# Four channel groups of a depthwise convolution moved from banded matmuls on TensorE to fp32 taps on VectorE

## The reference

```
def conformer_conv_branch(h, w_in, w_dw, b_dw, g_ln, b_ln, w_o):
    a, bgl, g = jnp.split(h @ w_in, 3, axis=-1)
    u = a * jax.nn.sigmoid(bgl)
    u = lax.conv_general_dilated(u, w_dw, window_strides=(1,), padding=[(CONV_PAD, CONV_PAD)], ...,
                                 feature_group_count=CONV_W) + b_dw
    u = jax.nn.silu(layer_norm(u, g_ln, b_ln)) * jax.nn.silu(g)
    return u @ w_o
```

## Time and profile before

| | us |
|---|---|
| median of 3 runs (lowest to highest) | 3001.74 (3001.47 to 3002.21) |
| span of the profiled execution | 2998.3 |
| its TensorE busy | 2915.5 |
| its VectorE busy | 1813.3 |
| its ScalarE busy | 1451.9 |
| its POOL busy | 426.1 |

### The profile page before, as it was taken

One profiled execution on the slowest core, in us unless ns is written; L12 is line 12 of the kernel. 1 busy time (PEld: TensorE's weight loads), 2 busy tenths in 40 slices (PEclk: granted clock), 3 DMA queues, 4 the chain that ended last, 5 costly groups with the idle time before them and its releaser, 6 DMA issues. The chain is left out here.

```text
span 2998.3 us, 44473 instructions
## 1 busy us (share of the span) xinstructions
PE 2915.5 (97%) x14789; PEld 2434.0 (81%) x14789; DVE 1813.3 (60%) x3147; ACT 1451.9 (48%) x3080; POOL 426.1 (14%) x491
## 2 busy tenths in 40 slices
PE   6999999999999999999999999999899999999898
PEld 4888888788888888888888888788788888888687
DVE  6555654567777677776767676733534444445875
ACT  5554645455555565656555565534512222222553
POOL 0000000022212221222122221200011111112000
PEclk9999999999999999999999999999999999999899
DMA  7657565611112111110212011145522222222563
GB/s 268 209 194 267 177 205 176 212 56 44 52 43 75 36 46 59 59 58 27 72 43 75 27 39 57 63 170 179 192 73 76 78 77 65 77 64 89 174 201 124
DMA packets 225865, 320.67 MB, mean 107 GB/s; under 512 B 81760, under 2 KB 143728, under 8 KB 224752
## 3 DMA queue, kind: packets, MB, share of 16 engines
q1 hardware_dynamic: 221040, 309.57, 31.7%
q10 hardware_dynamic: 4608, 8.39, 0.7%
HBM read 220.24 MB, written 97.66 MB: 106 GB/s over the span
## 5 line engine op out<-in xcount | busy, mean ns | idle before, releaser
L1309 DVE TENSOR_TENSOR at_ptlo<-at_T,at_pthi 128x512 fp32r<-128x512 f32 x576 | 396.6, 689 | 304.3 <-ACT at_pthi L1187 301.4
L1171 ACT ACTIVATE at_prob<-at_S,at_nmax 128x512 f32<-128x512 f32 x634 | 407.5, 658 | 341.4 <-DVE at_nmax L1285 334.5
L1187 ACT ACTIVATE at_pthi<-at_T 128x512 fp32r<-128x512 f32 x576 | 349.0, 608 | 210.1 <-PE at_T L1053 210.0
L1274 DVE TENSOR_REDUCE at_mx<-at_S 128x1 f32<-128x512 f32 x634 | 390.1, 629 | 73.2 <-PE at_S L1026 70.1
L1053 PE MATMUL at_T<-ident,at_prob 128*128 128x128 f32 x2304 | 346.1, 273 | 4.1 <-DVE at_ptlo L1309 4.1
L1053 PEld LDWEIGHTS at_T<-ident,at_prob 128*128 128x128 f32 x2304 | 279.4, 140 | 69.6 <-DVE at_ptlo L1309 12.8
L182 PE MATMUL ci_ps<-h1hi,ci_whi 128*128 128x512 f32 x768 | 300.2, 391 | 5.3 <-DVE h1lo L1970 5.3
L183 PE MATMUL ci_ps<-h1lo,ci_whi 128*128 128x512 f32 x768 | 299.7, 390 | 0.0
L184 PE MATMUL ci_ps<-h1hi,ci_wlo 128*128 128x512 f32 x768 | 299.4, 390 | 0.0
L182 PE MATMUL at_O<-at_pthi,at_vhi 128*128 128x512 f32 x576 | 270.1, 469 | 0.6 <-DVE at_og L1323 0.5
L1021 PE MATMUL at_S<-at_khi,at_qhi 128*128 128x512 f32 x634 | 245.3, 387 | 13.9 <-ACT at_prob L1171 10.9
(11 more groups left out here) (288 smaller groups left out, 6132.3 us busy)
## 6 DMA issues: line engine op xcount, KB each, us to landing
fr_w<-in_w_front SPq DMA_DIRECT2D x75, 512.0 KB, 4.4
at_wmod<-in_w_mod SPq DMA_DIRECT2D x32, 512.0 KB, 3.3
cv_w<-in_cv_w_in SPq DMA_DIRECT2D x24, 512.0 KB, 4.3
fr_w<-in_w_front SPq DMA_DIRECT2D x24, 384.0 KB, 4.1
values<-fr_ob SPq DMA_DIRECT2D x36, 256.0 KB, 3.2
at_vst<-values SPq DMA_DIRECT2D x8, 1152.0 KB, 7.0
fr_w_mod<-in_w_modr SPq DMA_DIRECT2D x17, 512.0 KB, 5.3
fr_x<-in_x SPq DMA_DIRECT2D x16, 512.0 KB, 6.8
```

The costliest lines, as they stand in the source:

```text
L1171: nc.scalar.activation(prob[:, j % 2, i, k], bank(h, j, i, c)[:, 0:k.stop - k.start], ACT.Exp, scale=SCALE, bias=nmax[:, i % 2:i % 2 + 1], ...
L1187: nc.scalar.activation(dst, T[:, (n + SLOTS * j) % 2], ACT.Copy).then_inc(s_hi, 1)
L1274: nc.vector.tensor_reduce(mx[:, i % 2, c:c + 1], bank(h, j, i, c)[:, 0:k.stop - k.start], AXX, ALU.max).then_inc(s_mx, 1)
L1309: nc.vector.tensor_tensor(ptlo[:, kt % 3], T[:, (n + SLOTS * j) % 2], pthi[:, kt % 3].bitcast(F32), ALU.subtract).then_inc(s_lo, 1)
```

## The change

Groups 0, 1, 3 and 4 (`TAPPED`) are no longer convolved by TensorE. Their u is loaded whole from DRAM into `ci_ut` (128 channels by 8 phases by 256 columns, with two columns of zeros on each side), and VectorE adds up 31 taps in `ci_acc`: one TENSOR_SCALAR for the first tap with the bias, then SCALAR_TENSOR_TENSOR, acc = u * weight + acc. A shift by a number of tokens that is no multiple of 8 wraps around the phases, so a tap is two instructions, together 2048 elements a partition. Each tap waits for the semaphore of the one before it. There are one `ci_ut` and one `ci_acc`.

`TAP_STEPS` deals out the 124 taps over the twelve steps of bodies 1 to 6: 20 or 21 a body, one or two a step, behind everything else that VectorE does in the step. A finished group is stored (`store_acc`), and the next is loaded directly behind (`load_rows`); the next group's first tap waits for both. The groups' sums are made in bodies 3, 4, 6 and 7 (`SUMMED_IN`), from rows reloaded from DRAM chunk by chunk (`reload_z`, `ci_zr`), with the same three operations as before.

Groups 2, 5, 6 and 7 (`BY_PE`) stay as they were, in bodies 3, 6, 7 and the tail of 7. Where a banded and a tapped group are summed in the same body, their sums alternate, and ScalarE's square stands between. `ci_gb` is gone: gates and u share `ci_ub`. All loops are written out. No other stage changes.

```
+TAPPED = (0, 1, 3, 4)
+SUMMED_IN = (3, 4, 6, 7)
+TAP_STEPS = [(g, s, n) for a, row in ((1, (1, 2, 2, 1, 2, 2, 1, 2, 2, 1, 2, 2)), (2, (1, 2, 2, 2, 2, 2, 1, 2, 2, 1, 2, 2)), (
+    3, (1, 2, 2, 1, 2, 2, 2, 2, 2, 1, 2, 2))) for g in (a, a + 3) for s, n in enumerate(row)]
...
+            def load_rows(i):
+
+                g = TAPPED[i]
+                for k in range(2):
+                    sp.wait_ge(s_ust[k], g * 32 + 32)
+                if i:
+                    sp.wait_ge(s_tap, i * CONV_K)
+                sp.dma_start(ut[:, :, HALO:HALO + NCOL], net.u_phases[g]).then_inc(s_ut, 16)
+
+            def store_acc(i):
+                sp.wait_ge(s_tap, (i + 1) * CONV_K)
+                sp.dma_start(net.z_phases[TAPPED[i]], acc[:]).then_inc(s_acc, 16)
+
+            def reload_z(i, q):
+
+                n = i * CH + q
+                if q == 0:
+                    sp.wait_ge(s_acc, 16 * (i + 1))
+                if n >= 2:
+                    sp.wait_ge(s_d, at[TAPPED[(n - 2) // CH], (n - 2) % CH] + 1)
+                sp.dma_start(zr[:, n % 2], net.z_chunks[TAPPED[i] * CH + q]).then_inc(s_zr[n % 2], 16)
+
+            def ended(g, s):
+
+                for i, when in ends.items():
+                    if when == (g, s):
+                        store_acc(i)
+                        if i + 1 < len(TAPPED):
+                            load_rows(i + 1)
...
+            def tap(n):
+
+                i, t = n // CONV_K, n % CONV_K
+                g = TAPPED[i]
+                shift, r = divmod(t - PAD, PHASES)
+                pieces = [(0, PHASES - r, r, HALO + shift)] + ([(PHASES - r, PHASES, r - PHASES, HALO + shift + 1)] if r else [])
+                if t == 0:
+                    dve.wait_ge(s_ut, 16 * (i + 1))
+                    if i:
+                        dve.wait_ge(s_acc, 16 * i)
+                else:
+                    dve.wait_ge(s_tap, n)
+                for a, b, d_s, d_n in pieces:
+                    z, u = acc[:, a:b], ut[:, a + d_s:b + d_s, d_n:d_n + NCOL]
+                    if t == 0:
+                        last = nc.vector.tensor_scalar(z, u, tw[:, g, 0:1], tb[:, g:g + 1], ALU.mult, ALU.add)
+                    else:
+                        last = nc.vector.scalar_tensor_tensor(out=z, in0=u, scalar=tw[:, g, t:t + 1], in1=z, op0=ALU.mult,
+                                                              op1=ALU.add)
+                last.then_inc(s_tap, 1)
...
                 for n in range(CH):
...
+                    if c is not None:
+                        if n + 1 < CH:
+                            band_and_low(c, n + 1)
+                        if n:
+                            banded_sums(c, n - 1)
...
                     if n % 2:
                         dve.wait_ge(s_ab, g * 8 + (n + 1))
+                        u_product(g, n // 2, ps[:, n % 6])
                     if n == 1:
                         w_low(g, G)
+                    if i is not None:
+                        tapped_sums(i, n)
+                    run_taps(g, n)
```

More of the change, by code:

```diff
@@ L1669, in conv_in @@
     CH = P // CCH
+    STEPS = 2 * NBLK + NBLK
+    BY_PE = tuple(g for g in range(GROUPS) if g not in TAPPED)
+    N_TAP = len(TAPPED) * CONV_K
     with nc.cleanup_on_exit(), ExitStack() as st:
@@ L1699, in conv_in @@
         NH = NBLK * KD
+        CONST = 64
         def home(b):
@@ L1722, in conv_in, with block_of, banded_group @@
         TAIL = ("G0", "G1", 0, 1, 2, "G2", 3, 4, 5, "G3", 6, 7)
[L1724 to L1733, removed]
+        def block_of(i, g=0):
+            return (i + NBLK - 1) % NBLK if g == 0 else i
+        def banded_group(g):
+            return g - 1 if g - 1 in BY_PE else None
@@ new lines, in nth @@
+        def nth(g, q):
+            return BY_PE.index(g) * CH + q
+        taps_at, ends = {}, {}
+        for g, s, n in TAP_STEPS:
+            taps_at[g, s] = n
+        done = 0
+        for g in range(GROUPS):
+            for s in range(STEPS):
+                for _ in range(taps_at.get((g, s), 0)):
+                    done += 1
+                    if done % CONV_K == 0:
+                        ends[done // CONV_K - 1] = (g, s)
+        assert done == N_TAP
+        first_tap = {}
+        done = 0
@@ new lines, in conv_in, with summed_group @@
+        for g in range(GROUPS):
+            for s in range(STEPS):
+                first_tap[g, s] = done
+                done += taps_at.get((g, s), 0)
+        def summed_group(g):
+            return next((i for i, b in enumerate(SUMMED_IN) if b == g), None)
+        sums = []
+        for g in range(1, GROUPS):
+            c, i = banded_group(g), summed_group(g)
+            for n in range(CH):
+                if c is not None and n:
+                    sums.append((c, n - 1))
+                if i is not None:
+                    sums.append((TAPPED[i], n))
+            if c is not None:
+                sums.append((c, CH - 1))
@@ L1772, in store_z @@
             def store_z(g, q):
[L1773 to L1780, removed]
-                for n in range(CH):
-                    if not first:
-                        reload_u(g - 1, n)
+                n = nth(g, q)
@@ new lines, in _ @@
+            for g in range(GROUPS):
+                c, i, last = banded_group(g), summed_group(g), g == GROUPS - 1
+                if g:
+                    ended(g - 1, STEPS - 1)
+                if g in BY_PE:
+                    if BY_PE.index(g):
+                        sp.wait_ge(s_tlo, BY_PE.index(g))
+                    sp.dma_start(taps[:], net.taps[g]).then_inc(s_taps, 16)
+                if i is not None:
+                    reload_z(i, 0)
+                for n in range(CH):
+                    if n:
+                        ended(g, n - 1)
+                    if i is not None and n + 1 < CH:
+                        reload_z(i, n + 1)
+                    if c is not None:
+                        reload_u(c, n)
@@ L1832, in h_high, with sigmoid @@
                 nc.scalar.activation(h_tile(hhi, n), h_tile(raw_h, n), ACT.Copy).then_inc(s_hhi, 1)
[L1834 to L1843, removed]
+            def sigmoid(g, n, src):
+                if g or n >= 2:
                     act.wait_ge(s_mul, g * 8 + (n - 1))
@@ L1971, in h_low @@
                                         ALU.subtract).then_inc(s_hlo, 1)
[L1973 to L1983 removed]
+            w_low(0, B)
@@ L2058, in gate @@
                 product(g, G, n % 6, b).then_inc(s_g, 1)
-            def body(g, first, last):
+            for g in range(GROUPS):
+                c = banded_group(g)
                 for b in range(NBLK):
@@ L2071, in body @@
                                 pe.wait_ge(s_mul, g * 8 + (b - 3 + 1))
-                        elif not first:
+                        elif g:
                             if n == 0:
```

314 lines of the change are left out of this document (178 added, 136 removed).

## The result

| | before | after |
|---|---|---|
| median of these runs, us | 3001.97 | 3019.49 |
| lowest to highest | 3001.47 to 3003.76 | 3015.88 to 3021.69 |
| span of the profiled execution | 2998.3 | 3018.0 |

The ratio is 1.0058, with an interval of 1.0046 to 1.0070: the change costs 17.5 us. The two profiled spans are 19.7 us apart.

A forecast was written before the change was run, and what follows sets the result against it. TensorE, busy 97% of the span, was taken to bound the kernel. VectorE's lateness 74 + clock 1.6 - 57.0 removed = +18.4 us; 2998.3 became 3016.7, and 3.4 for the runs' median gave 3020, range 2988 to 3042.

The forecast's parts named there:

- TensorE's work removed: Convolution stage: four of eight groups lose 32 convolutions of 1.78 us on TensorE, 57.0 us, all on the path.
- one tap (two pieces): VectorE, bodies 1 to 6: two pieces of 1.14 us plus 0.13 for the semaphore wait, 2.40 us.
- first tap of a group: VectorE's TENSOR_SCALAR opening each tapped group: 0.75 us per 1024 elements, some 1.35 us for two pieces.
- taps in the chain, undisturbed: VectorE, body 2 to body 7's first band: 100 taps at 2.40 plus three first ones at 1.35, 243 us.
- POOL beside VectorE, in the chain: Bodies 2 to 6: VectorE loses 1.1 us beside each of 18 ci_blo operations, 20 us.
- hand-overs: Bodies 2, 3 and 5: VectorE waits for a group's store and the next load, 10, 11 and 10, together 31 us.
- the whole chain: VectorE's work and waits from body 2's first A product to body 7's first band: 420 us, plus 2 us twice.
- lateness at body 7: Body 7's first convolution can start 435 us into body 2, against 361.6 for TensorE alone: 74 us late.
- clock behind that point: Body 7: after its wait TensorE restarts at the lower clock level, adding 1.6 us.
- cheap chain: Rival, VectorE's chain: free semaphore waits, lower-end transfers, average POOL cost; 2987 (chance 0.12), or 3007 with the first alone (0.10).
- Where TensorE waits: First convolutions of bodies 3, 6, 7: 12, 20, 15 us; before bodies 5, 6: 10, 5; later steps of 3, 6: 7.
- VectorE keeps up: Rival, convolution stage: TensorE stays the bound, -57 us, 2945; needs taps at about twice the rate; chance 0.03.

## Why the prediction was right, step by step

The time (3020 forecast, 3019.49 measured) and the mechanism hold: VectorE's chain from body 2 to body 7 sets the pace, and TensorE waits where bands and weight splits come late. The first convolution of body 7 is 74.0 us later than TensorE alone would be there (361.6 us behind the start of body 2); 73.8 had been worked out. That this number came out so well is in part luck, since errors cancel in it. So they do in the time: the forecast span was 3016.7 and the measured one is 3018.0, but the median of the runs lies only 1.5 us above it and not 3.4.

| step of the prediction | forecast | measured |
|---|---|---|
| TensorE's work removed | -57.0 | -56.4 to -57.6 (half-size taps) |
| one tap (two pieces) | 2.40 | 2.51 before another tap, 2.40 otherwise |
| first tap of a group | 1.35 | 2.38 |
| taps in the chain, undisturbed | 243 | about 251 |
| POOL beside VectorE, in the chain | 20 | about 17 |
| hand-overs | 10 + 11 + 10 | 9.7 + 8.2 + 7.7 |
| short waits for ScalarE and TensorE | 7 | 7.5 |
| products, splits, bands, sums | 123 | 123 |
| the whole chain | 424 | 424 |
| lateness at body 7 | 73.8 | 74.0 |
| clock behind that point | 1.6 | 2.6 |

The forecast of 7 is the 3 us for the squares and twice 2 us for late products; measured are six waits of 0.55 and two of 2.32 and 1.86. The measured terms are made from the distances between the starts of all VectorE records between 2289.57 and 2713.9 us: each group's own undisturbed distance times its count, and what is left over beside a POOL record or before a wait.

**Taps.** The term was off by 8 us: 5 in the taps and 1.03 in each of three first taps. The 2.40 for a tap holds two errors that cancel in part. A piece of 1024 elements takes 1.20 us to the next start and not the 1.14 of the earlier trace rows. Those two operations multiply by a constant and hand out a sum, while a tap takes its factor from SBUF, so they were not quite of the tap's kind; which difference costs the 0.06 no run shows. Against that, the semaphore's 0.13 is due only where a tap stands directly behind a tap, 51 of 103 times in the chain. For the first taps, the error was to take the rate of the earlier trace rows for pieces of another shape.

**The semaphore.** The 0.13 us taken from the earlier trace rows held up nearly: 2.51 against 2.40 in two pieces, 2.38 against 2.27 in one, 0.11 us where the next instruction waits for the tap. The rival "cheap chain" had this wait at nothing, and needed taps at 2.28; even those without the wait were at 2.40. (The Trainium skill, "VectorE: DVE Perf Modes", section "The DRAIN you can't avoid", says of eight copies in a row that the semaphore costs nothing extra. For operations of which each waits for the one before it, these rows speak against it.)

**POOL.** Direction right, price a little high: 1.1 us had been read from a single pair of records, while the run with small operations gives 0.94 for each of 16, and the chain's records about 17 us for 18. Fifteen VectorE records beside a `ci_blo` are 0.9 to 1.15 us longer than their kind elsewhere, three more 0.3 to 0.4.

**Hand-overs.** 25.6 instead of 31. By the median the store of 1 MB landed after 4.8 us (about 5 had been estimated) and the load after 7.3; at the first hand-over it was 6.3 and 9.2, which is why its wait is the longest:

```profile
z_phases<-ci_acc SPq DMA_DIRECT2D x3, 1024.0 KB, 4.8
ci_ut<-u_phases SPq DMA_DIRECT2D x3, 1024.0 KB, 7.3
```

The two overlap nearly completely, the lower end of my bounds. That the second would be the worst was wrong: its reload was issued at 2466.42, as soon as the store had landed, and came in 3.3 us later without queuing behind the load for long; the run with the sums in body 5 confirms that nothing was to be had there.

**Where TensorE waits.** Places as forecast, sizes near: body 3 12.5 (12), before body 5 7.2 (10), before body 6 2.4 (5), body 6 18.7 (20), body 7 14.0 (15), later steps of 3 and 6 6.1 (7). My list adds up to 69, not 74, and the measured waits only to 60.9. The step that failed is the clock: I had 4 us for it before body 7, where 10.8 were lost. That changed nothing in the total. VectorE decides when the band is ready, and a TensorE that is slower on its way there waits that much less. Only the loss behind the last forced wait is added to the time, 2.6 us against 1.6.

**The chances.** The rival "VectorE keeps up" was priced at 2945, and the half-size taps gave 2943.45, so its price was right and its condition, taps at twice the rate, was the one that the run had to create.

## What to carry to other kernels

Work moved to an idle engine should be added up from one deadline to the next and not over the whole stage: here three groups fit in sum, and 27 us hung on where two transfers, and the taps behind them, stood among the deadlines. Put a buffer's hand-over where other work is due anyway, well ahead of the next deadline, and price the work by its dependent start-to-start distance, in its own shape, beside the operations of POOL that it meets.

## What the runs showed of the hardware

A TENSOR_SCALAR in fp32 ran at two rates: 754 ns for 128x1024 and 1346 ns for 128x2048 in 8 rows of 256, but 2132 ns for 128x1792 in 7 rows of 256, both read out of rows of 260. (The Trainium skill, "VectorE: DVE Perf Modes", section "Mode 2×_2P — use both read ports for one tensor", asks for outermost dimensions that are even, or odd and equal for source and destination. Both sides have 7 rows here; the destination's rows lie end to end, so that it may count as one run of 1792, and then the rule agrees. No run here separates the two readings.)

After most stalls TensorE ran at the lower level for 3 to 5 us: 0.43 us between matmuls of 512 columns instead of 0.23, 0.21 between those of 256. Even the two stalls of 2.7 us within bodies 3 and 6 were followed by 3.3 us of it (2661.33 to 2664.68; the granted clock from 2661 to 2665 is 0.57). So a forced wait had an echo of 1.6 to 2.8 us lost. The length of the stall alone doesn't decide: behind the 2.43 us before body 6 the matmuls were 0.23 apart at once (2587.66 on; the granted clock from 2583 to 2592 is 1.00), behind the 2.44 us in body 7 they started 0.21 instead of 0.12 apart for 3.2 us. An echo lengthens a kernel whose next deadline is TensorE's own, and is free where another engine sets the deadline.
